# Expert steps of one 64-row block against steps of two 32-row groups on four column tiles

## The chip, the cores and the metric

One NeuronCore of a Trainium2 chip runs the whole layer as one program. The metric is device time in microseconds (us) of one execution, lower is better.

## The reference, cut to what matters

One layer of a hybrid encoder trunk in float32 for 512 tokens of width 1024: norm and input projection, retention and differential attention, output projection, then the routed mixture of experts that the change is about, a gated per-layer embedding and a last norm.

```
t = rmsnorm(x, norm_ffn)                                  # 512 x 1024
g_idx = argmax(t @ w_rg + b_rg)                           # 1 of 4 expert groups
le_sel = (t @ w_re + b_re)[its group's 4 experts]
top_v, top_i = top_k(le_sel, 2)                           # 2 of these 4 experts
combine = softmax(top_v) * softmax(group logits)[g_idx]
for each of 16 experts e:                                 # w_gate, w_up: 1024 x 512; w_down: 512 x 1024
    hid = silu(t @ w_gate[e]) * (t @ w_up[e])
    out += (hid * combine[:, e]) @ w_down[e]
x = x + out
x = x + sigmoid(rmsnorm(x) @ w_ple_gate) * (p @ w_ple_proj)
return rmsnorm(x)
```

Each token has two experts, so there are 1024 (token, expert) pairs. On the reference's own inputs its router gives the 16 experts 64, 53, 70, 61, 76, 72, 72, 62, 69, 67, 53, 61, 59, 57, 67 and 61 pairs.

## The kernel before, in words

**Ahead of the experts.** TensorE runs the projections in three passes of split float32, the attention and the output projection. DVE then computes the routing (`route`, L938 on): how many blocks of 64 rows each expert needs (L986 to L990), which token each row of each block is (L1004 to L1023), and two small tables, `blk_slot` and `blk_loads` (L1025 to L1029), that tell TensorE for each block in which slot of the weight ring its expert lies and how many loads of that slot it must have seen. With the counts above this makes 23 blocks: seven experts over 64 pairs take two, nine take one.

**The expert stage.** Weights come through a ring of three slots. One slot holds one expert: gate and up 4 MB in two halves of the contraction, down 2 MB. SP's queue reloads them in order (`reload`, L612): the first half of expert e waits until the last block of expert e-3 is past its first half of gate-up (`gu_half_done`), the second half waits for `gu_done`, the down weights for `dn_done`. After the last reload it issues the 4 MB of `w_ple_gate` (L627). Experts 0 to 2 are loaded ahead of the stage, 3 to 15 inside it.

**A block.** 64 tokens are gathered by POOL with an indirect DMA as 128 partitions of 512 numbers: partition 64q+t is half q of token t (`gather`, L660), with three row buffers and three blocks ahead. TensorE transposes them (`rows_transpose`, L1540, 4 transposes), ACT copies the result to `rowsT`. `gate_up` (L1547) then multiplies: for each of 8 pieces of the contraction two matmuls, one for each half q of the output columns (256 gate and 256 up), both with a stationary tile of 128x64 and 512 moving columns; q=0 writes PSUM partitions 0 to 63, q=1 64 to 127, so they lie on two column tiles of the array. ACT's `silu` and DVE's `hidden` make `hid`, TensorE transposes it (`hidden_transpose`, L1565, 2 transposes), DVE copies it to `hidT`, and `down` (L1571) multiplies with 4 pieces times 2 halves. DVE moves the result to `y_blk` (L1209) and POOL scatters it to `y_rows` with an indirect DMA (L677).

**Order on TensorE.** A step of the loop (L1593) is: hidden_transpose(b-1), gate_up(b), rows_transpose(b+1), down(b-1). Each float32 matmul stands in the trace as two MATMUL and two LDWEIGHTS records, so gate_up has 32 MATMUL records and down 16. `in_slot` (L1528) stands ahead of both: the sequencer loads two table entries to registers (L1530, L1531) and branches to one of three copies of the matmuls, one for each slot (L1532, L1535). The loop (`over_blocks`, L152) is unrolled three times on TensorE and runs 10 turns in any case; turns past the last block only compare and go on. Row buffers (L1596) follow from the unrolled index.

**After it.** Once the last y is out, SP loads the y rows back (L633), DVE splits the PLE gate weights (L1229) and adds the expert outputs to x (L1242), and TensorE does the gate product.

## Time and profile before

| | us |
|---|---|
| three runs, median (lowest to highest) | 660.85 (660.65 to 662.56) |
| the profiled execution, its own time | 661.52 |
| its span in the profile | 659.7 |
| mean granted TensorE clock | 0.968 |
| TensorE busy / weight loads busy | 614.5 / 389.2 |
| DVE / ACT / POOL busy | 215.6 / 202.3 / 59.8 |
| gate_up matmuls (L1556), busy | 165.2 |
| down matmuls (L1580), busy | 84.0 |
| moved by DMA | 153.34 MB, 232 GB/s over the span |

The expert stage runs from about 311 to 585 us of the span. Times in rows are us from the span's start. A timeline row is start, length, engine, line, operation, output<-inputs, count, and in brackets the idle time before it and what ended it. A window row is the stretch, its length, then busy us and number of instructions for PE, PEld, DVE, ACT and POOL, the granted TensorE clock, the DMA share and GB/s. "PEldq" are records of TensorE's sequencer (register and branch instructions), which no engine counts as busy.

### The profile page before, as it was taken

What the parts mean: (1) busy time and instruction counts of PE and PEld (TensorE: products, weight loads), DVE (VectorE), ACT (ScalarE), POOL (GpSimd) and SP (SyncE); (2) the same over time, 40 slices, a digit from 0 to 9 for tenths busy, and PEclk for the clock granted to TensorE, in tenths of its full rate; (3) what the DMA queues carried; (4) which work ended last, traced back from release to release, by engine and by line L of the source; (5) the groups of instructions that cost most, each with busy time, mean ns of one, the idle gap of its engine ahead of it and who ended that gap; (6) DMA issues with size and microseconds to landing.
All of it is one profiled execution on the core that took longest, in us unless ns stands there. A gap on an engine that the chain in (4) does not pass through costs nothing.

```text
span 659.7 us, 9372 instructions
## 1 busy us (share of the span) xinstructions
PE 614.5 (93%) x3378; PEld 389.2 (59%) x3379; DVE 215.6 (33%) x480; ACT 202.3 (31%) x440; POOL 59.8 (9%) x105
## 2 busy tenths in 40 slices
PE   6999999999999999996899999999999999935995
PEld 6998877879989899953233333333333333314883
DVE  3521265456253442365011110111111011165663
ACT  5532354545444533342110100101010010152674
POOL 0000000000000000002112212121221212110000
PEclk8999999999999999978899999999999999986998
DMA  8743114111111079854989999998998999955001
GB/s 311 210 153 128 64 65 128 64 65 65 65 65 65 1 262 393 311 224 155 330 322 398 398 394 397 382 343 294 395 397 326 379 399 396 406 217 204 32 33 64
DMA packets 76416, 153.34 MB, mean 232 GB/s; under 512 B 7960, under 2 KB 27296, under 8 KB 76128
## 3 DMA queue, kind: packets, MB, share of 16 engines
q1 hardware_dynamic: 72144, 139.77, 57.8%
q0 software_dynamic: 3952, 12.85, 5.1%
q8 instruction: 22, 0.36, 0.2%
q10 hardware_dynamic: 288, 0.28, 0.2%
q14 instruction: 10, 0.08, 0.0%
HBM read 142.66 MB, written 10.23 MB: 232 GB/s over the span
## 4 chain that ended last, share of the span: by engine, by line
PE 85%; DVE 5%; DMA 4%; ACT 2%; SPq 2%; issue 2%; DVEq 0%; POOLq 0%; POOL 0%; ACTq 0%
PE bank L1556 22%; PE bank L1296 13%; PE bank L1297 12%; PE bank L1298 12%; PE bank L1580 11%; PE bank L1378 2%; DMA ring_gu<-in_w_up 2%; PE bank L1503 2%; PE bank L1544 2%; SPq L577 2%; PE bank L1351 2%; DVE ple_lo L1229 2%; DMA gmix<-in_norm_mix 1%; PE bank L1568 1%; PE bank L1392 1%
## 5 line engine op out<-in xcount | busy, mean ns | idle before, releaser
L1556 PE MATMUL bank<-ring_gu,rowsT 128*64 128x512 f32 x736 | 165.2, 601 | 2.8 <-issue 1.7
L1556 PEld LDWEIGHTS bank<-ring_gu,rowsT 128*64 128x64 f32 x736 | 51.0, 138 | 100.8 <-issue 99.6
L1580 PE MATMUL bank<-ring_dn,hidT 128*64 128x512 f32 x368 | 84.0, 598 | 1.4 <-DVE hidT L1200 1.4
L865 ACT ACTIVATE silu_g<-bank 128x256 f32<-128x256 f32 x23 | 8.8, 383 | 236.5 <-PE bank L1556 236.5
L1045 DVE TENSOR_TENSOR w_lo<-w_raw,w_hi 128x2048 fp32r<-128x2048 f32 x18 | 41.3, 2292 | 76.8 <-ACT w_hi L730 69.6
L1195 DVE TENSOR_TENSOR hid<-silu_g,bank 128x256 f32<-128x256 f32 x23 | 9.7, 421 | 166.0 <-ACT silu_g L865 166.0
L1296 PE MATMUL bank<-w_hi,hT_hi 128*128 128x256 f32 x192 | 56.1, 292 | 0.8 <-issue 0.8
L1297 PE MATMUL bank<-w_lo,hT_hi 128*128 128x256 f32 x192 | 54.9, 286 | 0.0
L1298 PE MATMUL bank<-w_hi,hT_lo 128*128 128x256 f32 x192 | 54.8, 286 | 0.0
L1296 PE MATMUL bank<-hT_hi,w_hi 128*128 128x512 f32 x128 | 50.8, 397 | 0.0
L1580 PEld LDWEIGHTS bank<-ring_dn,hidT 128*64 128x64 f32 x368 | 24.4, 136 | 44.7 <-issue 44.7
L1297 PE MATMUL bank<-hT_lo,w_hi 128*128 128x512 f32 x128 | 49.9, 390 | 0.0
L1298 PE MATMUL bank<-hT_hi,w_lo 128*128 128x512 f32 x128 | 49.9, 390 | 0.0
L1209 DVE COPY y_blk<-bank 128x512 f32<-128x512 f32 x23 | 15.9, 692 | 78.1 <-PE bank L1580 78.1
L1296 PEld LDWEIGHTS bank<-w_hi,hT_hi 128*128 128x128 f32 x192 | 37.5, 195 | 2.1 <-issue 2.1
L1297 PEld LDWEIGHTS bank<-w_lo,hT_hi 128*128 128x128 f32 x192 | 37.5, 195 | 0.0
L1298 PEld LDWEIGHTS bank<-w_hi,hT_lo 128*128 128x128 f32 x192 | 37.4, 195 | 0.0
L730 ACT ACTIVATE w_hi<-w_raw 128x2048 fp32r<-128x2048 f32 x18 | 34.3, 1906 | 2.1 <-DMA w_raw<-in_w_in 2.1
L657 POOL COPY src_now<-src_row 128x1 int32 (+1 forms) x26 | 5.2, 199 | 312.6 <-DVE dst_row L1023 304.2
L1296 PEld LDWEIGHTS bank<-hT_hi,w_hi 128*128 128x128 f32 x128 | 24.0, 188 | 8.0 <-issue 3.3
L1296 PE MATMUL bank<-ple_hi,x2T_hi 128*128 128x512 f32 x64 | 26.0, 407 | 2.5 <-issue 2.5
L665 POOL DMA_INDIRECT rows<-h_rows,src_now x26 | 25.7, 990 | 20.7 <-POOL src_now L657 20.7
(210 smaller groups left out, 906.5 us busy)
## 6 DMA issues: line engine op xcount, KB each, us to landing
ring_gu<-in_w_gate SPq DMA_DIRECT2D x32, 1024.0 KB, 14.4
ring_gu<-in_w_up SPq DMA_DIRECT2D x32, 1024.0 KB, 15.3
ring_dn<-in_w_down SPq DMA_DIRECT2D x16, 2048.0 KB, 14.0
w_raw<-in_w_in SPq DMA_DIRECT2D x14, 1024.0 KB, 5.0
w_raw<-in_w_out SPq DMA_DIRECT2D x4, 1024.0 KB, 4.8
ple_gate_raw<-in_w_ple_gate SPq DMA_DIRECT2D x1, 4096.0 KB, 26.3
yg<-y_rows SPq DMA_DIRECT2D x8, 512.0 KB, 7.5
xr<-in_x SPq DMA_DIRECT2D x4, 512.0 KB, 9.2
```

The lines of the kernel that those rows point to most:

```text
L577: sp.dma_start(ring_gu[slot][:, ks, n, :], src[:, ks, :]).then_inc(s_gu[slot][half], 16)
L665: pool.indirect_dma_start(out=rows[buf][:], out_offset=None, in_=h2_rows, in_offset=rows_of).then_inc(s_rows[buf], 16)
L730: nc.scalar.activation(w_hi[u % 2][:], w_raw[u % 2][:], ACT.Copy).then_inc(hi_done, 1)
L1045: V.tensor_tensor(w_lo[u % 2][:], w_raw[u % 2][:], w_hi[u % 2][:].bitcast(F32), ALU.subtract).then_inc(lo_done, 1)
L1209: V.tensor_copy(y_blk[buf][:], b_dn[:]).then_inc(y_ready, 1)
L1229: V.scalar_tensor_tensor(ple_lo[q][:, k, :], ple_gate_raw[:, k, q * HALF:(q + 1) * HALF], gple[:, k:k + 1], ple_hi[q][:, k, :].bitcast(F32 ...
L1296: T.matmul(o, w_of(w[0], k), m_of(m[0], k), start=(k == 0), stop=False)
L1297: T.matmul(o, w_of(w[0], k), m_of(m[1], k), start=False, stop=False)
L1298: last = T.matmul(o, w_of(w[1], k), m_of(m[0], k), start=False, stop=(k == KD - 1))
L1351: last = T.matmul(b_score[2 * (i % 2) + c][:, 0:L], dqT[64 * c:64 * c + 64, h, i * P:(i + 1) * P], dkT[64 * c:64 * c + 64, h, 0:L], start= ...
L1556: last = T.matmul(b_gu[q * BLK:(q + 1) * BLK, :], rowsT[:, k % 4, k // 4, :], ring_gu[s][:, k, :, q * UC:(q + 1) * UC], start=(k == 0), st ...
L1580: last = T.matmul(b_dn[q * BLK:(q + 1) * BLK, :], hidT[:, kf % 2, kf // 2, :], ring_dn[s][:, kf, q * (D // 2):(q + 1) * (D // 2)], start=( ...
```

## The change

Groups of 32 rows take the place of blocks of 64, and a step works on two groups, which may belong to one expert or to two neighbours. Partition 64g+32q+t now is half q of token t of group g. `gate_up` issues four matmuls for each piece of the contraction (group g, half q), each with a stationary tile of 128x32 and 512 moving columns, on column tiles at partitions 0, 32, 64 and 96; `down` likewise. The weights that a matmul streams are those of its group's expert, so where both groups have one expert the same 512 columns are streamed for both. Where the groups have two experts, the matmuls wait for both slots.

An expert's last group is padded to 32 rows; the groups lie one behind the other, and a step ends wherever two are full. `cum_i` holds, for each expert, the step in which its last group is. Slots and load counts of both groups are packed in one number (`blk_code`), which `in_slots` loads once, takes apart with remainders and divisions, and branches on to one of six copies of the matmuls. TensorE's loop has one step in a turn and 24 turns; the row buffer comes from the turn by a branch. There are two row buffers, gathered two steps ahead. The gathers and scatters keep their shape (2 KB pieces), as do the weight loads (2 and 4 KB pieces). The empty rows now are gathered from a zero row pair behind `h2_rows`, written by a small DMA of SP. The routing tables change with it (50 group entries on one partition in place of 32, tables of 28 step columns in place of 34).

```diff
 TOP_K = 2
 NR = N_GROUPS + N_EXPERTS
 BLK = 64
-BPE = SEQ // BLK
-
-MAX_BLOCKS = (TOP_K * SEQ - N_EXPERTS) // BLK + N_EXPERTS
+ROW_BUFS = 2
+
+LOADS_0 = 8
+LOADS_1 = 64
+GPE = SEQ // GRP
 GROUP = 6
-PE_GROUP = 3
-TABLE = MAX_BLOCKS + ROW_BUFS
+
+MAX_GROUPS = (TOP_K * SEQ - N_EXPERTS) // GRP + N_EXPERTS
...
-            def gather(b, buf, n_columns):
-
-                rows_of = column(src_now[buf], src_row, b)
+            def gather(b, buf, now, n_columns):
+
+                rows_of = column(src_now[now], src_row, b)
                 pool.wait_ge(column_ready, n_columns)
                 pool.sem_inc(gathers_begun, 1)
                 pool.indirect_dma_start(out=rows[buf][:], out_offset=None, in_=h2_rows,
@@ -678,15 +688,15 @@
                                         in_offset=None).then_inc(s_ystored, 16)
             for b in range(ROW_BUFS):
-                gather(b, b, b + 1)
+                gather(b, b, b, b + 1)
             pool.wait_ge(xT_done, 1)
-            gather(ROW_BUFS, 0, ROW_BUFS + 1)
+            gather(ROW_BUFS, 0, ROW_BUFS, ROW_BUFS + 1)
             def step(b, k, turn):
                 pool.wait_ge(xT_done, b + 1)
-                gather(b + ROW_BUFS, (1 + k) % ROW_BUFS, 2 * b + ROW_BUFS)
+                gather(b + ROW_BUFS, (1 + k) % ROW_BUFS, k % 3, 2 * b + ROW_BUFS)
                 scatter(b - 1, k % 2, 2 * b + (ROW_BUFS + 1))
...
+                n_grp = 2 * MAX_BLOCKS
+                link(V.tensor_tensor(grp_ge[:], iota_blk[0:1, 0:n_grp].unsqueeze(2).to_broadcast([1, n_grp, 16]),
+                                     cum[0:1, :].unsqueeze(1).to_broadcast([1, n_grp, 16]), ALU.is_ge))
+                link(V.tensor_reduce(grp_e[:], grp_ge[:], X, ALU.add))
+
+                link(V.tensor_scalar(steps_f[:], cum[0:1, :], 0.5, 0.25, ALU.mult, ALU.add))
+                link(V.tensor_scalar(steps_r[:], steps_f[:], ROUND, None, ALU.add))
+                V.tensor_scalar(cum_i[:, 0:N_EXPERTS], steps_r[:], -ROUND, None, ALU.add)
+                link(V.tensor_scalar(cum_i[:, N_EXPERTS:], steps_r[:, N_EXPERTS - 1:], -ROUND - 1.0, None, ALU.add))
...
+                link(V.tensor_scalar(code[0][:], e_of[:, :, 1], float(RING), float(LOADS_0 + LOADS_1), ALU.mult, ALU.add))
+                link(V.scalar_tensor_tensor(code[1][:], e_of[:, :, 0], 1.0 - RING, code[0][:], ALU.mult, ALU.add))
+                link(V.scalar_tensor_tensor(code[2][:], q_of[:, :, 0], float(LOADS_0 - RING), code[1][:], ALU.mult, ALU.add))
+                V.scalar_tensor_tensor(blk_code[:], q_of[:, :, 1], float(LOADS_1), code[2][:],
+                                       ALU.mult, ALU.add).then_inc(table_ready, 1)
...
             pe.wait_ge(table_ready, 1)
-            total = pe.value_load(cum_i[0:1, N_EXPERTS - 1:N_EXPERTS], min_val=N_EXPERTS, max_val=MAX_BLOCKS)
-
-            def in_slot(b, products):
-
-                loads = pe.value_load(blk_loads[0:1, bass.ds(b, 1)], min_val=1, max_val=6)
-                slot = pe.value_load(blk_slot[0:1, bass.ds(b, 1)], min_val=0, max_val=RING - 1)
-                with pe.If(slot < 1):
-                    products(0, loads)
+            total = pe.value_load(cum_i[0:1, N_EXPERTS - 1:N_EXPERTS], min_val=N_EXPERTS // 2, max_val=MAX_BLOCKS)
+
+            def in_slots(b, products):
+
+                code = pe.value_load(blk_code[0:1, bass.ds(b, 1)], min_val=LOADS_0 + LOADS_1, max_val=8 * LOADS_1 - 1)
+                pair, loads = code % LOADS_0, [code // LOADS_0 % (LOADS_1 // LOADS_0), code // LOADS_1]
+                with pe.If(pair < RING):
+                    with pe.If(pair < 1):
+                        products((0, 0), loads)
+                    with pe.Else():
+                        with pe.If(pair < 2):
+                            products((1, 1), loads)
+                        with pe.Else():
+                            products((2, 2), loads)
                 with pe.Else():
-                    with pe.If(slot < 2):
-                        products(1, loads)
+                    with pe.If(pair < RING + 1):
+                        products((0, 1), loads)
                     with pe.Else():
-                        products(2, loads)
-
-            def rows_transpose(b, buf, loads):
+                        with pe.If(pair < RING + 2):
+                            products((1, 2), loads)
+                        with pe.Else():
+                            products((2, 0), loads)
+
+            def rows_transpose(buf, loads):
                 pe.wait_ge(s_rows[buf], 16 * loads)
                 for j in range(4):
@@ -1546,21 +1575,25 @@
             def gate_up(b):
-                def products(s, loads):
+                def products(slots, loads):
                     pe.wait_ge(xT_ready, b + 1)
                     for k in range(KD):
                         if k % (KD // 2) == 0:
-                            pe.wait_ge(s_gu[s][k // (KD // 2)], 32 * loads)
-                        for q in range(2):
-                            last = T.matmul(b_gu[q * BLK:(q + 1) * BLK, :], rowsT[:, k % 4, k // 4, :],
-                                            ring_gu[s][:, k, :, q * UC:(q + 1) * UC],
-                                            start=(k == 0), stop=(k == KD - 1))
+                            pe.wait_ge(s_gu[slots[0]][k // (KD // 2)], 32 * loads[0])
+                            if slots[1] != slots[0]:
+                                pe.wait_ge(s_gu[slots[1]][k // (KD // 2)], 32 * loads[1])
+                        for g in range(2):
+                            for q in range(2):
+                                o = g * BLK + q * GRP
+                                last = T.matmul(b_gu[o:o + GRP, :], rowsT[:, k % 4, g, k // 4, :],
+                                                ring_gu[slots[g]][:, k, :, q * UC:(q + 1) * UC],
+                                                start=(k == 0), stop=(k == KD - 1))
                         if k == KD // 2 - 1:
                             last.then_inc(gu_half_done, 1)
                     last.then_inc(gu_done, 1)
-                in_slot(b, products)
+                in_slots(b, products)
             def hidden_transpose(b):
                 pe.wait_ge(hid_ready, b + 1)
@@ -1570,33 +1603,40 @@
             def down(b):
-                def products(s, loads):
+                def products(slots, loads):
                     pe.wait_ge(hidT_ready, b + 1)
                     pe.wait_ge(y_ready, b + 1)
-                    pe.wait_ge(s_dn[s], 16 * loads)
+                    pe.wait_ge(s_dn[slots[0]], 16 * loads[0])
+                    if slots[1] != slots[0]:
+                        pe.wait_ge(s_dn[slots[1]], 16 * loads[1])
                     for kf in range(D_EXPERT // P):
-                        for q in range(2):
-                            last = T.matmul(b_dn[q * BLK:(q + 1) * BLK, :], hidT[:, kf % 2, kf // 2, :],
-                                            ring_dn[s][:, kf, q * (D // 2):(q + 1) * (D // 2)],
-                                            start=(kf == 0), stop=(kf == D_EXPERT // P - 1))
+                        for g in range(2):
+                            for q in range(2):
+                                o = g * BLK + q * GRP
+                                last = T.matmul(b_dn[o:o + GRP, :], hidT[:, kf % 2, g, kf // 2, :],
+                                                ring_dn[slots[g]][:, kf, q * (D // 2):(q + 1) * (D // 2)],
+                                                start=(kf == 0), stop=(kf == D_EXPERT // P - 1))
                     last.then_inc(dn_done, 1)
-                in_slot(b, products)
-
-            rows_transpose(0, 0, 1)
+                in_slots(b, products)
+
+            rows_transpose(0, 1)
             pe.wait_ge(ple_ready, 2 * NT)
             gate_up(0)
-            rows_transpose(1, 1, 1)
+            rows_transpose(1, 1)
             def step(b, k, turn):
                 hidden_transpose(b - 1)
                 gate_up(b)
-                rows_transpose(b + 1, (2 + k) % ROW_BUFS, PE_GROUP // ROW_BUFS * turn + ((2 + k) // ROW_BUFS + 1))
+                with pe.If(turn % ROW_BUFS < 1):
+                    rows_transpose(0, turn // ROW_BUFS + 2)
+                with pe.Else():
+                    rows_transpose(1, turn // ROW_BUFS + 2)
                 down(b - 1)
-            over_blocks(pe, total, step, group=PE_GROUP)
+            over_blocks(pe, total, step, group=1)
             hidden_transpose(total - 1)
             down(total - 1)
```

## Rows read from the trace of the kernel before

**Rows 1.** The page's part 2, the span in 40 equal slices.

```profile
PE   6999999999999999996899999999999999935995
DMA  8743114111111079854989999998998999955001
```

**Rows 2.** Timeline of PE alone, one block of the expert stage.

```profile
347.99 7.09 PE L1556 MATMUL bank<-ring_gu,rowsT 128*64 128x512 f32 x32
355.01 0.66 PE L1544 MATMUL bank<-small,rows 128*128 128x128 f32 x4
355.60 3.65 PE L1580 MATMUL bank<-ring_dn,hidT 128*64 128x512 f32 x16
359.19 0.44 PE L1568 MATMUL bank<-small,hid 128*128 128x128 f32 x2
359.55 0.65 PE L1556 MATMUL bank<-ring_gu,rowsT 128*64 128x512 f32 x2
```

**Rows 3.** Timeline of PE, matmuls of the same kind on the whole array.

```profile
297.63 5.31 PE L1503 MATMUL bank<-ple_proj,pT 128*128 128x512 f32 x12
```

**Rows 4.** Windows of the expert stage: busy us, clock, DMA share, GB/s.

```profile
335.00:340.00 5.00, 5.00 (x26) 1.63 (x24) 1.02 (x2) 0.00 (x0) 1.40 (x3) 1.00 0.61 173
340.00:425.00 85.00, 85.00 (x402) 28.55 (x398) 10.14 (x22) 7.24 (x15) 17.59 (x29) 1.00 1.04 396
425.00:515.00 90.00, 90.00 (x421) 30.15 (x422) 11.51 (x24) 7.46 (x15) 18.97 (x32) 1.00 0.95 350
515.00:584.00 69.00, 67.29 (x316) 22.51 (x314) 8.76 (x18) 5.88 (x12) 13.04 (x22) 1.00 1.03 394
```

**Rows 5.** Timeline of the end of the expert stage: PE, DVE and SP's queue.

```profile
548.49 1.08 PE L1556 MATMUL bank<-ring_gu,rowsT 128*64 128x512 f32 x4 [0.32 <-DMA ring_gu<-in_w_up]
...
581.18 3.65 PE L1580 MATMUL bank<-ring_dn,hidT 128*64 128x512 f32 x16 [1.39 <-DVE hidT L1200]
...
584.88 0.69 DVE L1209 COPY y_blk<-bank 128x512 f32<-128x512 f32 x1 [3.83 <-PE bank L1580]
585.49 10.68 DVE L1229 SCALAR_TENSOR_TENSOR ple_lo<-ple_gate_raw,gple,ple_hi 128x512 fp32r<-128x512 f32 x16
...
596.09 1.28 DVE L1242 SCALAR_TENSOR_TENSOR xr<-yg,w_top,xr 128x1024 f32<-128x1024 f32 x1
```

**Rows 6.** SP's DMAs of line 577, window 551.5 to 552: expert 15's last gate-up pieces.

```profile
L577 SPq DMA_DIRECT2D ring_gu<-in_w_up x1: 2507/2507/2507, 551.6 to 551.6; - x1
...
DMA to landing us min/median/max: 15.3/17.6/19.9
```

**Rows 7.** DMA issues on the page: count, KB each, us to landing.

```profile
rows<-h_rows,src_now POOLq DMA_INDIRECT x26, 6.2
y_rows<-y_blk,dst_now POOLq DMA_INDIRECT x23, 6.2
```

**Rows 8.** Records by line in narrow windows around 362 to 366 us (ns min/median/max, first to last).

```profile
L1532 PEldq COMPARE_BRANCH  x1: 178/178/178, 362.2 to 362.2; - x1
...
L1556 PE MATMUL bank<-ring_gu,rowsT x22: 592/592/592, 361.8 to 366.0; 128*64 128x512 f32 x22
...
L1530 PEldq FUSED_REGOPS  x2: 42/96/151, 363.1 to 363.6; - x2
...
L1576 PEldq ALU_OP  x1: 39/39/39, 365.4 to 365.4; - x1
```

**Rows 9.** The same view over the whole span: sequencer work of `in_slot` and the loop.

```profile
L1530 PEldq TENSOR_LOAD <-blk_loads x46: 301/312/773, 310.9 to 578.1; - x46
...
L1532 PEldq COMPARE_BRANCH  x62: 79/196/354, 312.2 to 581.3; - x62
...
L156 PEldq COMPARE_BRANCH  x10: 86/216/218, 355.7 to 577.8; - x10
```

**Rows 10.** Timeline of PE, the first block's gate_up.

```profile
312.75 9.02 PE L1556 MATMUL bank<-ring_gu,rowsT 128*64 128x512 f32 x32 [0.78 <-ACT rowsT L860]
```

**Rows 11.** DMA view, window 320 to 370: queues.

```profile
q8 instruction: 5, 0.08, 0.7%
```

98 lines of the change are left out of this document (51 added, 47 removed).

## Prediction

> **What bounds the kernel now.** I read the page's slices first [rows 1]: in the expert stage, slices 19 to 34, both TensorE and the DMA engines stand at 9 almost throughout. So the question is which of the two sets the end once one of them gets less to do. The timeline of a block [rows 2] answers for TensorE: block starts lie 359.55 - 347.99 = 11.56 us apart, made of 7.02 for gate_up, 0.59 and 0.36 for the transposes and 3.59 for down, without a gap. The 23 blocks at this pace are the stage. The windows [rows 4] answer for the DMAs: 396 GB/s from 340 to 425 with a share of 1.04 is their full rate, but between 425 and 515 they move less, since SP then waits for ring slots that TensorE has not given free. Over that stretch a rate of 350 where 396 is possible leaves (396 - 350) x 90 / 396 = 10.4 us unused. The dip at 335 to 340 (173) comes from the stage's start and stays, and from 515 to 584 the rate is 394. So that is all the reserve there is: TensorE is the bound today, and the weight stream stands about 10 us behind it. At 548.49 a gate_up already waits for weights [rows 5]. A change that speeds TensorE's part by more than this reserve is paid only up to it.
>
> **The number of steps.** With the pair counts of the router, groups of 32 are 2, 2, 3, 2, 3, 3, 3, 2, 3, 3, 2, 2, 2, 2, 3 and 2, together 39, so 20 steps in place of 23 blocks (the same counts give the 23 of the trace).
>
> **The array part of a step: unchanged.** A record of 512 columns takes the whole array 0.43 us: 12 in 5.31, less the 0.59 of the last, over 11 intervals [rows 3]. In gate_up 32 records take 7.09, so (7.09 - 0.59) / 15 = 0.43 for a pair [rows 2]: two column tiles run side by side at no cost. The change has twice the records on four tiles. If four overlap as two do, a round of four takes 0.43 again and a step's array part stays 11.56. Nothing in the trace shows four; the bounds are 0.43 for a round and 0.86 (two pairs one after the other). I take 0.43, since the second tile adds nothing measurable.
>
> **The sequencer's part.** Here the cover halves. At 362.2 the sequencer already stands at the branch behind gate_up's last matmul, while 22 records are still running or to come up to 366.0 [rows 8]; four are running, so it runs ahead by 18 records, nine pairs, 3.85 us. With four to a round the same 18 records are 4.5 rounds, 1.9 us. After gate_up the first matmul of down starts at 359.55 + 7.61 = 367.16 [rows 2], so cover falls from 4.96 to 3.0 us. The work under it now: 0.9 to the table load at 363.1, then 2.3 to the last register op at 365.4 [rows 8]. In the changed kernel: leaving the branch 0.2, row buffer by branch 0.5 and 0.2 to leave it, then in_slots: one load with its register ops 0.75 in place of 1.5, four to eight register ops more at 0.1, two or three branches at 0.2 with gap [rows 9], waits 0.2 to 0.3, so 2.0 to 2.5. In all 2.9 to 3.4 against 3.0: 0.1 us late. Between down and gate_up the cover is 1.9 + 0.95 = 2.85; the work is 0.2, the loop's turn, now in every step, 0.8 (its branch is 0.22 [rows 9]), and 2.0 to 2.5: 0.25 late. A step becomes 11.9 us. With all branches at their 0.35 maximum and loads at 0.77 [rows 9] it would be 13.7; below 11.56 it can't go.
>
> **TensorE's end.** The fourth block starts at 347.99, the 23rd starts 19 periods later, and its down ends at 584.88 [rows 5], 17.25 later. After: 16 steps from the fourth to the twentieth, two more ahead of it stretched, and the loop's turns past the last step: five empty ones before the last down where two stand now, some 0.65 each, 2.0 in all. So the end by TensorE alone is 347.99 + 2 x (S - 11.56) + 16 S + 17.25 + 2.0 = 344.1 + 18 S. With S = 11.9 that is 558.
>
> **The DMAs' end.** Expert 15's last gate-up piece was issued at 551.6 and landed 15.3 later, at 566.9 [rows 6]. What gets earlier: the 10.4 us of unused rate, for the slots now come free sooner, and the rows' traffic: three steps fewer at 2 x 0.262 MB and one look-ahead gather fewer [rows 7], 1.84 MB, 4.6 us at 396 GB/s. New landing: 551.9. It is needed in the middle of the 19th gate_up. Today's trace has the same place: at 548.49 block 21 went on after such a wait, and the last down ended 36.4 later with two blocks behind it. One block less: 24.8. Add the empty turns 2.0, the sequencer gaps 0.5, and the clock: the first gate_up took 9.02 after a pause, 1.9 more than 7.09 [rows 10]; the last steps now wait for weights (6.29 + 0.52 MB at 396 GB/s is 17.2 us for an expert, against 11.9 for its step), and whether such waits of 2 to 3 us cost clock isn't shown, so between 0 and 1.9, taken as 1.0. Sum: 551.9 + 24.8 + 2.0 + 0.5 + 1.0 = 580.2. This is later than 558, so the weight stream sets the end and most of the 35 us of three blocks turns into waits of TensorE for `ring_gu`.
>
> **The rest.** Routing: more entries on one partition, some eight short DVE operations more, partly under TensorE's wait for the gathered rows; 0.2 us later, at worst 1. Two row buffers: a gather lands in 6.2 us [rows 7] and is asked for two steps of 11.9 ahead, less half a step for the scatter in front of it on POOL; cost nothing; if it were late, the transposes would wait and S grow by it. SP waits for two first gathers, not three, and issues expert 2's down earlier: nothing, it isn't needed for four steps. The small zero-row DMA goes while SP waits for h2 anyway. The tail: the DVE split of 10.7 us starts behind the last y [rows 5], and the PLE gate weights land well ahead of it, so all behind the last down moves with it.
>
> **Sum.** 580.4 in place of 584.88: 4.5 us less. The profiled execution took 661.52 for a span of 659.7; it becomes 657.0. The median of the runs is 0.67 below the profiled one: **656.4**. About 0.3% (2 us) is what a measurement of this kernel can tell from no change.
>
> **Rivals.**
> 1. The DMA reserve is not recovered whole. Slots may come free no sooner in the steps with two experts, and a full rate of 390 in place of 396 alone costs 3.5 us over 235 us of stream. The end is 583 to 587: 659 to 663, within 0.3%. For it: the reserve is small. Chance 0.17.
> 2. The sequencer becomes the bound. It has its place ahead of both matmul groups, and decides from S = 13.1 (344.1 + 18 S = 580.2), 1.2 us over my 11.9. At the bound of 13.7: 590.7, 5.8 more than today, 666.6. For it: half the cover, three nested branches; against: one load fewer. Chance 0.15.
> 3. Four tiles don't overlap wholly. From a round of 0.48 us on (1.2 us over 24 rounds) TensorE is the bound; at the pairwise bound of 0.86 a step is 22.2 and the kernel 820. A quarter of the way between the bounds, a round of 0.54, gives S = 14.5, 605 and 681. The rows speak against it, two tiles cost nothing. Chance 0.10. The Trainium skill speaks for it (TensorE: Matmul & The Clock Gate, Part 3 on packing): three column tiles of 32 measured 2.38 times one, not 3. By that ratio, 0.79, a round would be 0.54 us. No run here shows it, and for two tiles the trace shows the full factor.
> 4. Instructions are fetched late. Between 320 and 370 five instruction packets of 16 KB came [rows 11], later in the loop none, so the three unrolled steps stay resident; the new loop holds six copies of both groups, a third more. If it no longer fitted, one load a step at a gather's 6.2 us gives S = 18 and 744. Chance 0.03. The Trainium skill (Runtime: NRT & Kernel Launch, Instruction fetch mechanics) says that a branch out of a window of two pages forces a fetch. The trace disagrees for the present loop, whose 864 matmul records and loads span more than two such packets by that section's count and cause none.
>
> **Chances and range.** The forecast, 652 to 659, has 0.55, of which 0.02 falls within 0.3%. Faster 0.53, same 0.18 (with rival 1 and an edge of rival 2), slower 0.29. The range is 651 to 672: the low end takes a rate of 400 and no clock loss, the high end the sequencer's case with some room; rivals 3 and 4 are mostly left out.
>
> **What would show it.** Right: 1280 MATMUL records for gate_up and 640 for down, in rounds of four each 0.43; step periods of 11.9 until about step 14, then waits for `ring_gu` by DMA of 2 to 3 us, twice a step; a DMA rate near 396 from 340 on without the dips; last gate-up landing near 552; last down ending near 580. Wrong: rounds longer than 0.48, waits put down to "issue" ahead of gate_up or down of more than 1 us in every step, or dips of the DMA rate that stay.

## The result and the profile after

The changed kernel takes 668.26 us (median of 4 runs, 666.04 to 671.63) against 660.75 in the same comparison: a ratio of 1.0112, with an interval of 1.0084 to 1.014. It is slower by 1.1%, where 656.4, faster by 0.7%, was forecast; 668.3 lies within the range of 651 to 672.

The profiled execution took 666.24 for a span of 664.4. One thing has to be known before traces are compared: the first gate_up of the stage starts near 309 in some executions and near 313 in others, whatever the kernel. Most of the difference lies ahead of the stage: the same 12 records of the PLE product take 5.42 us in the profile after and 7.93 in the profile before, and the granted clock from 280 to 310 us is 0.97 and 0.88. The profile after has the early start (308.80), the one before the late one (312.75, [rows 10]). Counted from the first gate_up, the stage and what follows take 355.6 us after and 346.95 before, so this pair of profiles shows a loss of 8.7 us; the medians show 7.5. Counting from there doesn't take the clock out altogether. The kernel sp_before (below) differs from the one before only in the order of its reloads and has the same time, but its profile has the early start, and then the slow stretch of the clock falls into the first two gate_ups:

```profile
308.78 10.03 PE L1559 MATMUL bank<-ring_gu,rowsT 128*64 128x512 f32 x32 [0.92 <-ACT rowsT L863]
...
322.02 8.54 PE L1559 MATMUL bank<-ring_gu,rowsT 128*64 128x512 f32 x32 [1.77 <-issue]
```

It needs 351.2 us from its first gate_up on. Differences of 2 to 4 us between two single profiles can be of this kind.

The slices of the page after, in 40 parts of 16.6 us:

```profile
PE   6999999999999999996469999998997878935995
...
PEclk8999999999999999998689999999998888985998
DMA  8733213111111089665909999999999999925001
GB/s 310 233 137 117 80 65 110 64 63 65 64 64 64 1 322 395 269 267 190 334 4 364 398 396 398 396 398 396 396 398 394 395 395 395 371 81 206 33 32 64
```

Against [rows 1] two things are new. In slice 20 (332 to 349 us) the DMAs stand still, 4 GB/s, and TensorE has holes there and in the slice ahead of it. And from slice 21 to 34 the DMAs stand at 9 throughout, with 394 to 398 GB/s from 365 to 565 us, and TensorE at 8 and 7 in places late in the stage. Before, TensorE had the nines.

The timeline of PE at the start of the stage (start, us, line, operation, count, idle time ahead and who ended it):

```profile
307.27 0.66 PE L1573 MATMUL bank<-small,rows 128*128 128x128 f32 x4 [4.34 <-DMA rows<-h_rows,src_now]
308.80 8.40 PE L1589 MATMUL bank<-ring_gu,rowsT 128*32 128x512 f32 x64 [0.87 <-ACT rowsT L870]
321.54 0.94 PE L1573 MATMUL bank<-small,rows 128*128 128x128 f32 x4 [4.34 <-issue]
322.27 0.63 PE L1601 MATMUL bank<-small,hid 128*128 128x128 f32 x2
327.73 9.17 PE L1589 MATMUL bank<-ring_gu,rowsT 128*32 128x512 f32 x64 [4.83 <-issue]
338.08 0.65 PE L1573 MATMUL bank<-small,rows 128*128 128x128 f32 x4 [1.18 <-issue]
342.72 5.07 PE L1617 MATMUL bank<-ring_dn,hidT 128*32 128x512 f32 x32 [3.98 <-issue]
347.72 0.44 PE L1601 MATMUL bank<-small,hid 128*128 128x128 f32 x2
348.09 7.07 PE L1589 MATMUL bank<-ring_gu,rowsT 128*32 128x512 f32 x64
355.09 0.66 PE L1573 MATMUL bank<-small,rows 128*128 128x128 f32 x4
355.68 3.64 PE L1617 MATMUL bank<-ring_dn,hidT 128*32 128x512 f32 x32
359.25 0.44 PE L1601 MATMUL bank<-small,hid 128*128 128x128 f32 x2
359.62 7.07 PE L1589 MATMUL bank<-ring_gu,rowsT 128*32 128x512 f32 x64
```

From 348.09 on the step is what was hoped for: 359.62 - 348.09 = 11.53 us, 64 records in 7.07, without a hole. But the first two steps have four holes put down to "issue", 14.3 us together, and the third gate_up starts 39.3 us behind the first; two blocks of the kernel before take 23.7, with holes of 1.7 (its second gate_up, below) and 0.4.

```profile
324.88 7.09 PE L1556 MATMUL bank<-ring_gu,rowsT 128*64 128x512 f32 x32 [1.68 <-issue]
```

So 12.2 of the 15.6 us that the third gate_up is later are holes. Most of the rest is clock: behind the holes of 4.83 and 3.98 us the second gate_up takes 9.17 instead of 7.07 and the first down 5.07 instead of 3.64, 3.5 us together.

"Issue" means that no semaphore and no other engine ended the wait. Only the sequencer's own records tell what it did. The view by line, branches alone, for lines 1553, 1556 and 1633 in narrow windows from 300 to 345, and for line 1553 from 350 to 580 (ns min/median/max, first to last start):

```profile
L1553 PEldq COMPARE_BRANCH  x3: 73/4292/7010, 308.2 to 323.0; - x3
...
L1556 PEldq COMPARE_BRANCH  x1: 3451/3451/3451, 334.2 to 334.2; - x1
...
L1633 PEldq COMPARE_BRANCH  x2: 81/1570/3058, 337.8 to 338.1; - x2
...
L1553 PEldq COMPARE_BRANCH  x32: 65/211/218, 354.4 to 576.0; - x32
```

Four branches in the first two steps last 7.0, 4.3, 3.5 and 3.1 us, 17.8 in all; the same lines stay under 0.22 from 350 to 580. One more of 3.4 us stands at 586.5, under the last down. Before, none of 62 went over 0.35 [rows 9]. In each of the four a 16 KB packet of the instruction queue starts while the branch stands, and the branch ends 2.3 to 2.9 us behind the start of the last one. Eight such packets come between 314 and 346 (five before, [rows 11]), and none from there to 587.

What this does to the weights stands in the windows (busy us by engine, clock, DMA share, GB/s), after; the last row is the 40 us from the first gate_up on:

```profile
310.00:330.00 20.00, 10.83 (x78) 3.31 (x74) 0.84 (x2) 1.06 (x3) 1.16 (x2) 0.76 0.98 362
330.00:350.00 20.00, 14.84 (x114) 4.10 (x110) 1.44 (x3) 0.98 (x2) 0.35 (x2) 0.86 0.09 21
350.00:425.00 75.00, 75.00 (x670) 23.04 (x664) 8.76 (x19) 6.30 (x14) 16.31 (x27) 1.00 1.04 394
425.00:515.00 90.00, 81.36 (x702) 24.27 (x702) 9.99 (x21) 6.46 (x13) 16.64 (x28) 0.98 1.04 396
...
308.80:348.80 40.00, 25.67 (x180) 7.42 (x184) 2.20 (x5) 3.23 (x6) 2.13 (x3) 0.80 0.51 187
```

and the first two windows and the last one before:

```profile
310.00:330.00 20.00, 16.28 (x66) 5.84 (x68) 0.85 (x2) 3.06 (x5) 3.79 (x7) 0.83 0.84 294
330.00:350.00 20.00, 20.00 (x96) 6.79 (x94) 2.89 (x6) 1.96 (x4) 2.89 (x6) 1.00 0.92 335
...
312.75:352.75 40.00, 37.91 (x168) 12.76 (x170) 3.73 (x8) 4.30 (x8) 6.89 (x11) 0.95 0.93 334
```

Between 310 and 350 the kernel before moves (294 + 335) x 20 = 12.6 MB, the changed one 7.7: 4.9 MB or 12.4 us of stream less, at 396 GB/s. Counted from each one's first gate_up, which takes out the early start of the profile after, it is (334 - 187) x 40 = 5.9 MB or 14.8 us. From 425 to 515 it moves (396 - 350) x 90 = 4.1 MB more, 10.5 us, as forecast. The first eats the second. At the end of the stage the timeline of PE shows who waits for whom:

```profile
557.53 5.18 PE L1589 MATMUL bank<-ring_gu,rowsT 128*32 128x512 f32 x32 [2.20 <-DMA ring_gu<-in_w_up]
563.61 3.64 PE L1589 MATMUL bank<-ring_gu,rowsT 128*32 128x512 f32 x32 [0.89 <-DMA ring_gu<-in_w_up]
...
571.71 7.08 PE L1589 MATMUL bank<-ring_gu,rowsT 128*32 128x512 f32 x64
...
585.62 3.64 PE L1617 MATMUL bank<-ring_dn,hidT 128*32 128x512 f32 x32 [1.01 <-DVE hidT L1220]
```

Expert 15's last piece lets the 19th gate_up go on at 563.6, and the last down ends at 589.3 (584.88 before, [rows 5]). The page's group for gate_up sums the waits, of which only 0.3 us were there before [rows 5]:

```profile
L1589 PE MATMUL bank<-ring_gu,rowsT 128*32 128x512 f32 x1280 | 152.7, 628 | 25.1 <-DMA ring_gu<-in_w_up 19.4
```

### The profile page after: what moved, and what is told of

Read it like the earlier page. It is cut to its first block, busy times and chain, and to the rows that moved or that the text cites. A ratio compares the mean times of both kernels' runs of the same rounds, so it can differ in the third digit from the quotient of the medians.

```text
span 664.4 us, 10864 instructions
## 1 busy us (share of the span) xinstructions
PE 587.1 (88%) x4176; PEld 369.8 (56%) x4177; DVE 212.8 (32%) x476; ACT 199.1 (30%) x434; POOL 51.6 (8%) x91
## 3 DMA queue, kind: packets, MB, share of 16 engines
q1 hardware_dynamic: 72176, 139.77, 56.9%
## 4 chain that ended last, share of the span: by engine, by line
PE 68%; SPq 11%; DMA 9%; DVE 6%; issue 4%; ACT 2%; DVEq 0%; POOLq 0%; POOL 0%; ACTq 0%
PE bank L1589 13%; PE bank L1316 12%; PE bank L1317 12%; PE bank L1318 12%; SPq L585 9%; PE bank L1617 7%; DMA ring_gu<-in_w_up 7%; PE bank L1398 2%; PE bank L1371 2%; DVE ple_lo L1249 2%; PE bank L1573 1%; DMA gmix<-in_norm_mix 1%; SPq L588 1%; PE bank L1412 1%; PE bank L1485 1%
## 5 line engine op out<-in xcount | busy, mean ns | idle before, releaser
L1589 PE MATMUL bank<-ring_gu,rowsT 128*32 128x512 f32 x1280 | 152.7, 628 | 25.1 <-DMA ring_gu<-in_w_up 19.4
L1589 PEld LDWEIGHTS bank<-ring_gu,rowsT 128*32 128x32 f32 x1280 | 40.8, 115 | 122.9 <-issue 101.4
L1617 PE MATMUL bank<-ring_dn,hidT 128*32 128x512 f32 x640 | 74.2, 605 | 5.0 <-issue 4.0
L1617 PEld LDWEIGHTS bank<-ring_dn,hidT 128*32 128x32 f32 x640 | 19.0, 111 | 45.6 <-issue 45.6
L1229 DVE COPY y_blk<-bank 128x512 f32<-128x512 f32 x20 | 13.8, 692 | 74.8 <-PE bank L1617 74.8
L1318 PEld LDWEIGHTS bank<-hT_hi,w_lo 128*128 128x128 f32 x128 | 24.0, 188 | 5.1
```

The costliest lines, as they stand in the source:

```text
L1229: V.tensor_copy(y_blk[buf][:], b_dn[:]).then_inc(y_ready, 1)
L1318: last = T.matmul(o, w_of(w[1], k), m_of(m[0], k), start=False, stop=(k == KD - 1))
L1589: last = T.matmul(b_gu[o:o + GRP, :], rowsT[:, k % 4, g, k // 4, :], ring_gu[slots[g]][:, k, :, q * UC:(q + 1) * UC], start=(k == 0), stop ...
L1617: last = T.matmul(b_dn[o:o + GRP, :], hidT[:, kf % 2, g, kf // 2, :], ring_dn[slots[g]][:, kf, q * (D // 2):(q + 1) * (D // 2)], start=(kf ...
```

## Experiments

Theory A: the first pass through the larger code is what costs. The sequencer jumps to instructions that have not come yet, stands there, TensorE gives the ring slots free late, the stream starts late, and since the stream sets the end it never makes that good. Theory B: the stream is late because of the two-expert steps themselves, whatever the start.

The table gives each kernel's profile; the three columns of times are in us behind the start of the first gate_up, so that the 4 us ahead of the stage drop out; what the clock did inside the first steps is in them. "Records" are the matmuls and weight loads that stand in the code of the loop, and of the gate_up ahead of it.

| kernel | records, loop + ahead | packets at the start | 3rd gate_up | 5th gate_up | rest of the span | median |
|---|---|---|---|---|---|---|
| before | 864 + 192 | 5 | 23.7 | - | 346.95 | 660.75 to 661.31 |
| after | 1152 + 768 | 8 | 39.3 | 62.4 | 355.6 | 668.26 |
| lean_peels | 1152 + 256 | 6 | 32.4 | 55.5 | 349.3 | 663.68 |
| one_body | 1152 + 0 | 5 | 36.4 | 59.7 | 356.05 | 668.99 |
| dry_turn | 1152 + 0 | 4 + 5 | 37.5 | 61.2 | 353.75 | 669.49 |
| whole | 864 + 576 | 6 | 33.1 | 56.2 | 351.75 | 666.27 |
| whole_lean | 864 + 192 | 5 | 29.6 | 52.7 | 345.2 | 660.89 |
| whole_lean_hint | 864 + 192 | 5 | 30.4 | 53.5 | 347.3 | 661.70 |
| mixed_first | 864 + 192 | 5 | 33.4 | 56.5 | 351.0 | 665.57 |
| hinted | 1152 + 768 | 10 | 30.3 | 62.4 | 356.2 | 672.61 |
| sp_after | 1152 + 768 | 8 | 45.4 | 68.4 | 359.0 | 671.75 |
| sp_whole_lean | 864 + 192 | 5 | 33.8 | 56.9 | 343.8 | 659.49 |
| sp_before | 864 + 192 | 5 | 26.2 | - | 351.2 | 661.56 |

### Is the stream the bound? half_down

```diff
-                sp.dma_start(ring_dn[slot][:],
-                             w_down[bass.ds(e, 1)].rearrange("o (k p) f -> p (o k) f", p=P)).then_inc(s_dn[slot], 16)
+                ks = slice(0, D_EXPERT // P // (1 if isinstance(e, int) else 2))
+                src = w_down[bass.ds(e, 1)].rearrange("o (k p) f -> p (o k) f", p=P)
+                sp.dma_start(ring_dn[slot][:, ks, :], src[:, ks, :]).then_inc(s_dn[slot], 16)
```

> The changed kernel with half of each reloaded down matrix left out (the other half of the product uses what lies there): 13 MB less to move. Theory A: behind the start TensorE is not waited for by anything but weights, so with 13.6 MB (34 us of stream) less the waits for ring_gu go, all steps behind the third take 11.53, and the last down ends near 348.1 + 17 x 11.53 + 17.6 = 561.7 instead of 589.3: 638 to 642. If the steps themselves (four tiles on two slots, clock) had got slower late in the stage, the end is over 570 and the time over 647.

648.28 us, a ratio of 0.9798 (0.978 to 0.9817). The code is the changed kernel's, and so are the long branches (6.2, 4.5, 3.4, 3.0 us). Window and last down of its profile:

```profile
425.00:515.00 90.00, 90.00 (x800) 27.58 (x792) 10.53 (x22) 7.84 (x16) 18.50 (x31) 1.00 1.03 386
```

```profile
566.41 5.34 PE L1618 MATMUL bank<-ring_dn,hidT 128*32 128x512 f32 x32 [1.01 <-DVE hidT L1221]
```

TensorE is busy all 90 us, at 11.5 us a step, up to the 18th. With the stream relieved, the stage is 22 us shorter from the first gate_up on (333.6 against 355.6). The medians differ by 20.0, where 26 to 30 were forecast: the profile began 4.4 us later than the one it was reckoned from, and the 18th and 19th step still waited (12.2 and 13.6 us). Behind the start, then, it is the weights that cost, and the steps themselves are sound.

### Fewer copies ahead of the loop: lean_peels, one_body

```diff
-            def in_slots(b, products):
+            def in_slots(b, products, only=None):
...
+                if only is not None:
+                    with pe.If(pair < 1):
+                        products((0, 0), loads)
+                    with pe.Else():
+                        products(only, loads)
+                    return
...
-            gate_up(0)
+            gate_up(0, (0, 1))
...
-            down(total - 1)
+            down(total - 1, (2, 0))
```

> Theory A (first pass through the code): the changed kernel loses its time where TensorE's sequencer jumps over copies whose instructions have not come yet (branches of 7.0, 4.3, 3.5 and 3.1 us between 314 and 341), so the reloads start late, the DMAs stand idle from 330 to 348, and the weight stream, which is the bound afterwards, never makes that good. Here the gate_up ahead of the loop and the down behind it have two copies instead of six, so their exit jumps pass 8 KB of instructions, not 40. The 7.0 us branch falls to under 1.5, the second gate_up starts near 322.5 instead of 327.7, the last down moves 4 to 7 us earlier, and the time is 659 to 664. Theory B (the stream alone): the stream is late because the two-expert steps give slots free late, whatever the start; the start may move but the end stays, 666 to 671.

663.68, a ratio to before of 1.0031 (1.001 to 1.0053): 4.6 us won by taking out code that never runs. The 7.0 us branch behind the first gate_up is 0.46 here (first row), but one of the loop's grew to 6.2:

```profile
L1559 PEldq COMPARE_BRANCH  x1: 460/460/460, 322.9 to 322.9; - x1
...
L1562 PEldq COMPARE_BRANCH  x3: 65/214/6197, 323.4 to 344.0; - x3
...
L1559 PEldq COMPARE_BRANCH  x3: 65/222/3599, 336.1 to 343.7; - x3
```

The third gate_up comes 6.9 us earlier, the end 6.3. This is the first evidence for A: the same work, the same transfers, another start.

one_body takes both groups into the loop, with guards for the first and last turn:

```diff
-            gate_up(0)
-            rows_transpose(1, 1)
...
-            over_blocks(pe, total, step, group=1)
-            hidden_transpose(total - 1)
-            down(total - 1)
+            with pe.Fori(0, MAX_BLOCKS) as turn:
+                with pe.If(turn < total + 1):
+                    with pe.If(0 < turn):
+                        hidden_transpose(turn - 1)
+                    with pe.If(turn < total):
+                        gate_up(turn)
...
+                    with pe.If(0 < turn):
+                        down(turn - 1)
```

> The first gate_up and the last down are put into the loop, so each matmul group stands six times in the code and not twelve (some 75 KB in place of some 150), at the price of three more branches a step. Theory A: all pages of the loop come during the first turn; the second gate_up starts near 325 to 328 as now, but the third 11.6 us behind it, near 339, instead of 348.1; the end moves 8 us earlier, 657 to 662. Theory B: unchanged, 666 to 671. If the added branches show, steps of over 11.6 us in the steady part.

668.99, 1.0105: a miss. Only five packets come, but the two jumps over whole groups of copies in the first turn cost 6.3 and 7.1 us. Fewer instructions are not enough; it is the far jumps in the first turn that stand.

### More code in the kernel before: pad_before, pad_before2

```diff
-                slot = pe.value_load(blk_slot[0:1, bass.ds(b, 1)], min_val=0, max_val=RING - 1)
+                slot = pe.value_load(blk_slot[0:1, bass.ds(b, 1)], min_val=0, max_val=2 * RING - 1)
...
-                        products(2, loads)
+                        with pe.If(slot < RING):
+                            products(2, loads)
+                        with pe.Else():
+                            for s in range(RING):
+                                products(s, loads)
```

> The kernel before with three more copies in each place that picks a ring slot, never run (six copies of 4 and 2 KB in place of three). Theory A: its sequencer now meets jumps over 12 to 20 KB in the first blocks, stalls of 3 to 7 us appear there, 8 or 9 instruction packets come instead of 5, and the end moves by the stalls, 5 to 12 us: 666 to 673. Theory B: code that never runs costs nothing, 660 to 662. Should the loop (some 110 KB) no longer stay resident, packets come in every block and it is over 700.

pad_before (the same without its first line) came out as 661.63, 1.0005 (0.9991 to 1.0018), with 22 packets as before. The bound of 2 on the slot had made the new branch constant, so the copies were not in the program: this run says nothing about either theory.

> The kernel before with three more copies, never run, in each place that picks a ring slot; in pad_before the program had dropped them, since the slot's bound of 2 made the branch to them constant, and its profile had the branches and the 22 packets of the kernel before, so it was that kernel again. Now the slot's bound is 5 and they stay in. Theory A (instructions that are jumped over are fetched too, a 16 KB packet each, and the sequencer stands until they are there): some 115 KB of loop and 24 KB ahead of it, so 8 or 9 packets in the first steps in place of 5, branches of 3 to 7 us, and TensorE's end moves by the stalls beyond what is queued: 5 to 12 us, 666 to 673. Theory B: code that never runs costs nothing, 660 to 662.

746.02 us, 1.1314 (1.1274 to 1.1354). Nothing that runs was changed. The page's instruction queue and the branches of the loop, from 300 to 660:

```profile
q8 instruction: 85, 1.39, 0.8%
```

```profile
L1532 PEldq COMPARE_BRANCH  x60: 71/293/5776, 308.7 to 655.6; - x60
...
L156 PEldq COMPARE_BRANCH  x9: 224/6224/7848, 363.6 to 659.7; - x9
```

The loop of 1728 records does not stay: between 363 and 408, one turn of three blocks, nine packets come, and the branch back to the loop's head has a median of 6.2 us. This is rival 4 of the prediction to the letter, at a size that the changed kernel (1152) does not reach. The expectation of pad_before had this as the remote case, the one of pad_before2 did not name it, so its range of 666 to 673 failed; its direction did not. For theory A's first pass this kernel is no test, since packets come all the time.

### Load the code ahead of time: dry_turn

The loop is entered behind the PLE products, and its first turn jumps over both groups with `pe.If(0 < turn)` and `pe.If(1 < turn)`; the routing's small matmuls stand between the two jumps.

> The changed kernel with one set of copies, in a loop that is entered earlier: its first turn runs no step and jumps over both matmul groups while the PLE products (16 records queued, 6.9 us) and later the wait for the rows (5 us) cover it, with the small matmuls of the routing put between the two. Theory A: the five packets come between 292 and 308 instead of 314 to 346, no branch over 1 us is left behind the first gate_up, the second and third gate_up start 11.7 and 23.3 us behind the first (now 18.9 and 39.3), the DMAs have no empty 16 us, and the end is 15 us earlier less what the stream then allows: 652 to 659, below the kernel before. If the first jump outlasts its cover, the routing moves by what is over, up to 5 us, and with it all behind: 657 to 664. Theory B (the stream alone): the start moves and the end stays, 666 to 671.

669.49, 1.0123, where 652 to 664 was expected: a miss that teaches. Branches of the dry turn (first two rows) and of the first real one:

```profile
L1630 PEldq COMPARE_BRANCH  x1: 6155/6155/6155, 296.0 to 296.0; - x1
...
L1642 PEldq COMPARE_BRANCH  x1: 4486/4486/4486, 302.5 to 302.5; - x1
...
L1553 PEldq COMPARE_BRANCH  x2: 65/2581/5097, 313.2 to 320.2; - x2
...
L1642 PEldq COMPARE_BRANCH  x1: 7112/7112/7112, 326.2 to 326.2; - x1
```

The dry jumps were covered as planned, and four packets came. Then line 1642 made the same jump again 24 us later and stood longer than the first time, with five more packets in the first real turn. Two packets start under either jump; under the first the DMAs moved 25 GB/s, under the second, with the weights on their way, 386. What a dry turn brings was not kept, while what a full turn brings stays for the whole stage. Why is open; no run here tells.

### Half the code for one-expert steps: whole, whole_lean

Where both groups have one expert, their 64 rows are one stationary operand again (the row order is q before g throughout):

```diff
+                        whole = slots[0] == slots[1]
+                        for g in range(1 if whole else 2):
+                            w = slice(0, 2) if whole else slice(g, g + 1)
...
-                                o = g * BLK + q * GRP
-                                last = T.matmul(b_gu[o:o + GRP, :], rowsT[:, k % 4, g, k // 4, :],
+                                o = q * BLK + g * GRP
+                                last = T.matmul(b_gu[o:o + (BLK if whole else GRP), :],
+                                                rowsT[:, k % 4, k // 4, w, :].rearrange("p g t -> p (g t)"),
```

> The changed kernel, but where both groups of a step have one expert their 64 rows are one stationary operand, as in the kernel before: the three copies (0,0), (1,1) and (2,2) have 32 and 16 matmuls instead of 64 and 32 at the same time on the array, and the loop falls from some 78 to some 60 KB. Nothing else changes. If what counts is how many instructions the first steps jump over and load (theory A as it stands now, with the two padded kernels and the dry turn behind it: pages are loaded when a jump needs them, and are kept only once the loop has been gone through), stalls fall by a quarter to a third of the 18 us of long branches, the third gate_up starts 32 to 36 us behind the first instead of 39.3 to 40.5, and the time is 4 to 8 us under the changed kernel's 668: 660 to 664. Theory B (the stream alone): 666 to 671, since what TensorE does and what is moved are the same.

> The same with two copies only ahead of the loop and behind it, as in lean_peels: some 12 KB there and 60 in the loop, about the 66 of the kernel before. Theory A: nearly its start, the third gate_up 24 to 29 us behind the first (kernel before 23.7, lean_peels 32.4), the DMAs idle under 5 us after the first reload, and then the forecast of the prediction holds: the stream sets the end some 4 us ahead of the kernel before, 654 to 660. Theory B: 663 to 671.

whole: 666.27, 1.0072 (1.0049 to 1.0095), the third gate_up at 33.1; the start moved as expected, the time less than expected (660 to 664). whole_lean: 660.89, 1.0000 (0.9976 to 1.0024): the whole loss is gone, but no gain came, and the forecasts of 654 to 660 and of a third gate_up at 24 to 29 (29.6) were just missed. It has exactly as many records in its code as the kernel before, and five packets too. What is left are two long branches that the kernel before has not; its exits pass at most 128 records and these 448 and 256:

```profile
L1562 PEldq COMPARE_BRANCH  x4: 65/142/3897, 319.6 to 343.2; - x4
...
L1559 PEldq COMPARE_BRANCH  x5: 65/217/3324, 319.2 to 342.9; - x5
```

### Hints and order: hinted, whole_lean_hint, mixed_first

```diff
+                            ahead = pe.mark_branch_hint_location()
                             products(slots[c], loads)
+                            pe.br(f"{name}_end").branch_hint(ahead)
```

For this the nest of `pe.If` is written out as explicit branches, with the copies in the same order.

> The changed kernel, all twelve copies kept, with one instruction more at the head of each copy: a hint to the instruction fetch where the copy's last branch will go. That place can then be loaded while the copy's matmuls are issued (7 us in gate_up). Theory A: only the timing of the instruction fetch differs, so the long exit branches (7.0 and 3.5 us in the profile after) fall under 1 us, the branches into copies (4.3, 3.1) stay in part; the third gate_up starts 28 to 34 us behind the first instead of 39.3 to 40.5, and the time is 6 to 10 under the 668 of the change: 658 to 663. Theory B: no change, 666 to 671, or slower by what the hints cost in every step. Should hints have no effect on the chip, the long branches are all there and the time is 668.

> whole_lean with the same hints in its twelve copies of the loop. Its profile had two long branches left, both exits of copies (3.9 and 3.3 us), and its third gate_up 29.6 us behind the first. Theory A: both go, the third gate_up starts 23 to 26 us behind the first, and the time falls from 660.9 to 655 to 658, below the kernel before. If the stream already binds so hard that 5 us at the start are worth nothing: 660 to 661.

hinted: 672.61, 1.0178 (1.0154 to 1.0202), 4 us above the changed kernel where 6 to 10 below it were expected. The exit branches did fall (7.0 to 2.2, 3.5 to 2.2 us) and the third gate_up came at 30.3. But packets came again from 356 to 375, another branch stood 5.9 us at 353, and the fifth gate_up starts at 62.4, just as without hints. What was won was given back in the next two steps. Why packets come there, in a loop that needs none in the other kernels, is open. In whole_lean_hint (661.70, 1.0007; 655 to 658 was expected) the two long branches are unchanged, 3.9 and 3.3 us: no effect that a profile shows.

mixed_first puts the copies for two experts ahead of those for one:

> whole_lean with the copies in another order in both places: first the three for two experts (24 and 12 KB), then the three for one expert (12 and 6 KB), so that in the first steps, which all have one expert, the exit branches are short, and the long way is the branch into the copy. Theory A (a stall for each jump to code not yet there): one long branch is left ahead of the second gate_up, partly covered by the first one, and none behind it until the first two-expert step; the third gate_up starts 25 to 28 us behind the first instead of 29.6, and the time is 657 to 660 against 660.9. If jumps into copies stall as the exits did, both matmul groups are hit and it stays at 660 to 662. Theory B: unchanged.

665.57, 1.0071 (1.0045 to 1.0098), 4.7 us slower than whole_lean by order of code alone, and outside both expected ranges. As expected one long branch is left, the one into the copies; the second row is the instruction queue from 324.63 to 331.46, while it stands:

```profile
L1558 PEldq COMPARE_BRANCH  x2: 449/3642/6835, 324.6 to 339.9; - x2
...
q8 instruction: 1, 0.02, 1.0%
```

but it lasts 6.8 us with one packet, where the two of whole_lean last 3.9 and 3.3, with one each, and stand partly under queued matmuls. Here TensorE stands idle for 8.1 us, and the gate_up behind that hole takes 10.08 us instead of 7.09.

So the number of packets doesn't set the length of a branch. The traces of the kernels with groups of 32 agree on what does. Where a packet starts under a long branch, the branch ends 2.3 to 2.9 us behind the start of its last packet (3.5 where two start within 0.8 us of each other). What varies is how long the packet takes to start: with little other traffic (under 80 GB/s) branches with one packet last 3.0 to 3.7 us, with the weight stream running (over 290 GB/s) 3.8 to 6.8.

### Which way does it reach the end: sp_after, sp_whole_lean, sp_before

SP's waits in the profile after, 300 to 420 us (waited for, us in total, times, longest):

```profile
SPq L588 <- PE bank L1617: 41.8, 4, 29.4
```

SP stands 29.4 us for the first down, which ends at 347.8 (not 347.2, as the expectation below has it), while the first half of expert 1's slot is free from 333.5 on; in the kernel before its longest such wait is 12.0. So the reloads were put into the order in which slots come free:

```diff
-            def reload(e, slot):
+            def reload_gu(e, slot):
...
+            reload_gu(RING, 0)
             with sp.Fori(0, N_EXPERTS // RING - 1) as turn:
                 for slot in range(RING):
-                    reload(RING * turn + (RING + slot), slot)
-            reload(N_EXPERTS - 1, 0)
+                    reload_gu(RING * turn + (RING + 1 + slot), (slot + 1) % RING)
+                    reload_dn(RING * turn + (RING + slot), slot)
+            reload_dn(N_EXPERTS - 1, 0)
```

> The changed kernel with only the order of SP's reloads altered: an expert's down matrix is reloaded behind the next expert's gate and up matrices, not ahead of them, which is the order in which TensorE gives the slots free. TensorE's code and its long branches stay. Theory A2 (the stalls cost through SP): with the late first down (it ends at 347.2 in the profile after), SP stands 29.4 us at that one wait while slots of expert 1 are free from 332.9 and 336.3 on; that is the empty stretch of the DMAs. Expert 4's 4.2 MB now go there, the stream is 8 to 10 us ahead from then on, and as it sets the end, the time is 659 to 663 with the long branches unchanged. Theory A1 (the stalls cost through TensorE's own lateness): what was lost at the start stays lost, 666 to 671.

> whole_lean (660.9) with the same order of reloads. Theory A2: its longest wait of SP at a first down is 19.1 us, some 5 to 8 us of them empty of transfers, and they are won: 652 to 656, below the kernel before. Theory A1: 660 to 661.

> The kernel before with the same order of reloads. TensorE sets its end in 23 blocks without a gap, so a stream that is further ahead is worth nothing: 660 to 662, with the DMA rate nearer 396 before 425 and more unused rate behind it. If it is faster by more than 1 us, the weights had cost it something after all.

sp_after: 671.75, 1.0166 (1.0136 to 1.0195), slower still and above both ranges. The hole in the stream did fill, from 21 to 224 GB/s, but look at the branches at the same places of the code (3.5 and 3.1 us in the profile after):

```profile
330.00:350.00 20.00, 10.22 (x72) 3.02 (x68) 0.42 (x1) 0.98 (x2) 0.00 (x0) 0.67 0.61 224
350.00:425.00 75.00, 75.00 (x654) 22.67 (x650) 9.69 (x20) 5.89 (x12) 14.42 (x25) 0.98 0.85 321
```

```profile
L1559 PEldq COMPARE_BRANCH  x1: 5881/5881/5881, 334.4 to 334.4; - x1
...
L1636 PEldq COMPARE_BRANCH  x2: 83/2920/5758, 340.4 to 340.7; - x2
```

5.9 and 5.8 us. With weights in the queues the instruction packets start 3.5 and 3.3 us into the branch instead of 1.1 and 0.2, the third gate_up falls back by another 6 us, and the stream stands at 321 GB/s later instead. sp_whole_lean shows both sides as well: its second long branch is 6.2 us instead of 3.3, and yet it is the shortest from the first gate_up on (343.8); its median of 659.49 is 0.999 of before (0.997 to 1.001), no difference, where 652 to 656 was expected by A2. sp_before: 661.56, 1.0008, none either, as expected; its DMA rate is not, for ahead of 425 us it falls (396 in the same window before):

```profile
350.00:425.00 75.00, 75.00 (x354) 25.28 (x352) 9.08 (x19) 6.87 (x14) 15.21 (x25) 1.00 0.98 369
```

So theory A2 holds for the hole itself and fails for the time: filling the hole lengthens the branches. Part of the lower rate later may also come from the new order itself, as in sp_before; the two are not separated.

## Why the prediction was wrong, step by step

**Steps and array: right.** 20 steps; 1280 and 640 records; a round of four tiles 0.43 us (64 records in 7.07). Rival 3 is out. The Trainium skill (TensorE: Matmul & The Clock Gate, Part 3) has 2.38 for three column tiles; the trace has the full factor for four.

**Sequencer in the steady part: too dear.** Forecast were 0.35 us of gaps a step, measured none (11.53, even under the 11.56 before). From the exit of gate_up's copy at 352.43 the sequencer reaches down's copy at 354.96: 2.5 us of work, where 2.9 to 3.4 were put against a cover of 3.0. Rival 2 is out too.

**Unused rate: right.** The stream runs at 396 from 425 to 515, the 10.5 us are won. Its price for an expert, 17.2 us, is the period of three late steps (197.1, 214.3, 231.5, 248.7 behind the first gate_up).

**The start: the step that failed.** The prediction took the first steps over unchanged: "the dip at 335 to 340 comes from the stage's start and stays", and reckoned the landing from it. The first pass of the sequencer through the new code had no term in the sum; it stood 17.8 us at four branches there. In place of a dip to 173 for 5 us came 20 us at 21, 12.4 us of stream in all. Put that term in: 551.9 + 12.4 = 564.3, and expert 15's last piece was there at 563.6. (All of these are times of the spans, so the early start of the profile after is inside the 12.4 us.) With the forecast's own 28.3 us from there to the end it would be 592.6; the last down ended at 589.3, as that leg took 25.7: its allowances for empty turns, gaps and clock, 3.5 us, were mostly not needed.

**Rival 4: the right mechanism at the wrong place.** It asked whether the new loop stays resident, and priced that it does not, at 0.03. It does stay. What it left out is the first pass: five packets in 50 us [rows 11] were read as harmless because no branch before passed 0.35 us. The likely reason that they were harmless is one that the change removes: a copy's exit passed at most 128 records, and now up to 640. The Trainium skill (Runtime: NRT & Kernel Launch, Instruction fetch mechanics) has the rule that a taken branch to what is not loaded must wait for its page. The traces agree for first visits (3 to 7 us) and disagree with a window of two pages: a loop of 1152 records ran 230 us without a packet, while one of 1728 kept loading them. The same section counts 256 instructions to 16 KB, and by that the packets of the table come out as records / 256, rounded up: 1920 gives 8, 1408 gives 6, 1056 gives 5. Two kernels don't follow: hinted has 10, and dry_turn has 4 ahead of its 5. Register instructions are left out of this count.

**Clock.** Taken as 1.0 us. Halves of late gate_ups took 5.27 and 5.18 instead of 3.64 behind waits of 2 to 3 us, at a mean granted clock of 0.93 from 515 to 585. After each of the two, TensorE still waited for weights (1.60 and 0.89 us), and behind 563.61 all runs at 7.08 and 3.64, so in this profile they cost the end nothing that shows. At the start the clock does cost, about 3 of the 15.6 us that the third gate_up is later (3.5 behind the holes, less 0.6 for a faster first gate_up); the forecast had no term for this. The slow matmuls stand behind the holes, but no run changes the one without the other.

**How firm is theory A?** Over the nine kernels with groups of 32 and the old order of reloads (half_down aside), the fifth gate_up ranges from 52.7 to 62.4 and the rest of the span from 345.2 to 356.2: a microsecond late at the start is about a microsecond late at the end (a line through the nine has a slope of 1.0, and they lie within 2.4 us of it), whether copies were removed, shrunk or only put in another order. Theory B asked for the same end in all. one_body lies 2.3 us above that line, which its added branches or the clock may or may not explain. The fifth gate_up counts holes and slow clock together, so the line shows that lateness at the start costs, and the branch records show where most of it comes from. What was not found is a version that beats the kernel before: three steps fewer on TensorE, 35 us of work, are worth nothing while the weights set the end.

## What to carry to other kernels

When a change multiplies the copies of code behind a branch, count the instructions that its first pass must jump over, and look at the sequencer's branch records, not only at matmul counts: a far jump costs 3 to 7 us once, more of it while other transfers run, and a loop too large costs it every turn. If the stage is bound by a stream that goes on when the first steps give buffers free, as here, those few microseconds go to the end undiminished. And leave out copies that cannot occur: keeping two of six ahead of the loop and behind it gave 4.6 us back.

## What the runs showed of the hardware

- A branch to code that is not loaded stands 3.1 and 3.5 us with empty DMA queues and 5.8 and 5.9 with the weight stream running (after against sp_after, same places); over all kernels with groups of 32, 3.0 to 3.7 with under 80 GB/s of other traffic and 3.8 to 6.8 us with over 290, each with one packet. It ends 2.3 to 2.9 us behind the packet's start.
- A loop of 1152 matmul and load records stays loaded on TensorE; one of 1728 loads nine packets in the turn from 363 to 408 us and costs 85 us in all.
- A turn that only jumps over the code does not make it stay (dry_turn).
- Branch hints shortened two exits from 7.0 and 3.5 to 2.2 us in one kernel, which became 4 us slower all the same, and did nothing in the other.
- Matmuls behind long holes ran slow: a gate_up behind 4.83 us took 9.17 instead of 7.07 (after), one behind 8.14 us 10.08 instead of 7.09 (mixed_first).
- Four column tiles of 32 rows run side by side in the time of two of 64: 0.43 us a round.
